# Wider column groups, a fifth buffer for high parts and later half tiles in the expert stage of an encoder kernel

## The reference, cut to what matters

```python
def _swiglu(h, w_gate_up, w_down):           # D_FF = 3584
    gu = h @ w_gate_up                       # [1024, 7168]: gate columns, then up columns
    g, u = gu[..., :D_FF], gu[..., D_FF:]
    return (jax.nn.silu(g) * u) @ w_down     # [3584, 1024]

for e in range(N_EXPERTS):                   # 8 experts
    y = y + gate_full[..., e:e + 1] * _swiglu(h, w_gate_up[e], w_down[e])
```

## Time and profile before

| | us |
|---|---|
| median of 3 runs (lowest, highest) | 1522.66 (1520.52, 1523.55) |
| the profiled execution | 1522.17 |
| its span | 1520.2 |
| TensorE busy | 1481.3 |
| VectorE busy | 1158.3 |
| ScalarE busy | 991.1 |

### The profile page before, as it was taken

One profiled execution on the slowest core, in us unless ns is written; L12 is line 12 of the kernel. 1 busy time (PEld: TensorE's weight loads), 2 busy tenths in 40 slices (PEclk: granted clock), 3 DMA queues, 4 the chain that ended last, 5 costly groups with the idle time before them and its releaser, 6 DMA issues.

```text
span 1520.2 us, 19543 instructions
## 1 busy us (share of the span) xinstructions
PE 1481.3 (97%) x7678; PEld 1208.7 (80%) x7678; DVE 1158.3 (76%) x1021; ACT 991.1 (65%) x869; POOL 132.2 (9%) x137
## 2 busy tenths in 40 slices
PE   8999999999989999999999999999999999999996
PEld 6888888899969987888777788777888777888774
DVE  5555445454565456899899988899898999898997
ACT  5544434343453337777798777888776888776986
POOL 0000000006034314000000200000100000000000
PEclk9999999999999999999999999999999999999999
DMA  9655555567516653899999999999999999999996
GB/s 333 214 170 190 168 192 171 189 192 224 194 57 213 206 185 126 329 356 355 366 405 417 398 407 405 395 408 415 399 408 403 395 408 415 399 404 408 393 391 220
DMA packets 151056, 468.26 MB, mean 308 GB/s; under 512 B 9856, under 2 KB 15872, under 8 KB 138416
## 3 DMA queue, kind: packets, MB, share of 16 engines
q1 hardware_dynamic: 144784, 453.93, 79.8%
q0 software_dynamic: 2816, 9.96, 2.3%
q10 hardware_dynamic: 3360, 3.06, 0.7%
HBM read 459.55 MB, written 7.37 MB: 307 GB/s over the span
## 4 chain that ended last, share of the span: by engine, by line
PE 79%; DVE 13%; ACT 3%; DMA 1%; SPq 1%; issue 1%; DVEq 0%; ACTq 0%
DVE wlo L418 9%; PE bS L437 6%; PE bS L438 6%; PE bS L436 6%; PE bY L436 6%; PE bY L438 6%; PE bY L437 6%; PE bG L436 4%; PE bG L438 4%; PE bU L436 4%; PE bG L437 4%; PE bU L438 4%; PE bU L437 4%; DVE wlo_more L418 2%; ACT whi L412 2%
## 5 line engine op out<-in xcount | busy, mean ns | idle before, releaser
L418 DVE TENSOR_TENSOR wlo<-raw,whi 128x2048 fp32r<-128x2048 f32 x364 | 827.2, 2296 | 179.6 <-ACT whi L412 178.4
L412 ACT ACTIVATE whi<-raw 128x2048 fp32r<-128x2048 f32 x364 | 692.3, 1915 | 262.1 <-PE bS L438 118.2
L418 DVE TENSOR_TENSOR wlo_more<-raw_more,whi 128x2048 fp32r<-128x2048 f32 x60 | 136.4, 2288 | 10.7 <-ACT whi L412 10.6
L412 ACT ACTIVATE whi<-raw_more 128x2048 fp32r<-128x2048 f32 x60 | 114.5, 1914 | 28.0 <-DMA raw_more<-in_m_w_gate_up_dram 8.4
L1086 PE MATMUL bY<-whi,hTh 128*128 128x512 f32 x224 | 91.5, 408 | 6.9 <-DVE wlo L418 4.9
L436 PE MATMUL bY<-whi,hTh 128*128 128x512 f32 x224 | 89.8, 401 | 0.0
L437 PE MATMUL bY<-whi,hTl 128*128 128x512 f32 x224 | 89.1, 398 | 0.0
L437 PE MATMUL bS<-whi,eTl 128*128 128x512 f32 x192 | 76.4, 398 | 0.0
L436 PE MATMUL bS<-whi,eTh 128*128 128x512 f32 x192 | 76.4, 398 | 0.0
L1086 PE MATMUL bS<-whi,eTh 128*128 128x512 f32 x192 | 76.3, 398 | 0.0
L1087 PE MATMUL bY<-wlo,hTh 128*128 128x512 f32 x184 | 73.2, 398 | 0.0
(11 more groups left out here) (536 smaller groups left out, 3336.4 us busy)
## 6 DMA issues: line engine op xcount, KB each, us to landing
raw<-in_m_w_gate_up_dram SPq DMA_DIRECT2D x184, 1024.0 KB, 14.5
raw<-in_m_w_down_dram SPq DMA_DIRECT2D x90, 1024.0 KB, 14.4
raw_more<-in_m_w_gate_up_dram SPq DMA_DIRECT2D x40, 1024.0 KB, 14.6
raw<-in_b_w_in_dram SPq DMA_DIRECT2D x36, 1024.0 KB, 5.1
raw<-in_f_w_gate_up_dram SPq DMA_DIRECT2D x28, 1024.0 KB, 5.2
raw_more<-in_m_w_down_dram SPq DMA_DIRECT2D x20, 1024.0 KB, 14.2
raw<-in_f_w_down_dram SPq DMA_DIRECT2D x14, 1024.0 KB, 5.0
raw<-in_a_w_out_dram SPq DMA_DIRECT2D x4, 1024.0 KB, 16.8
```

The costliest lines, as they stand in the source:

```text
L412: nc.scalar.activation(whi[:, h], raw_of(r), ACT.Copy).then_inc(hi_done, 1)
L418: nc.vector.tensor_tensor(wlo_of(r), raw_of(r), whi[:, h].bitcast(F32), ALU.subtract).then_inc(lo_done, 1)
```

## The change

Five edits go together, all in the expert stage.

1. **Groups of 2048 columns.** The 7168 columns are taken in order: three groups of 8 tiles, each tile 128 rows x 2048 columns (rows of 8 KB), into four banks G, S0, S1, U at once, then 4 tiles of 256 rows x 1024 columns (rows of 4 KB) into G and S0. Gate slabs 0 to 3 come from group 0, gates 4 to 6 and up 0 from group 1, ups 1 to 4 from group 2, ups 5 and 6 from the narrow tiles. Gates wait in a new area `parked` (over `hTl`). At each group change all four banks have to be evicted, each for itself (`gu_psum`, `column_sums`, `bank_free`), before PE writes it again.
2. **A fifth high buffer** `whi_late` (over `hn`, which is free by then), used from the seventh tile of item 0 on. `LEAD` = 4 takes the place of `CUT` = 3: splits run four tiles ahead.
3. **Evictions** stand in ACT's program behind the split at t = 6, 14, 22 (and 27), not behind t = 7, 15, 23.
4. **Turns** of slabs 0 to 6 stand in PE's program behind tiles 17, 24, 25, 27, 29, 31, 33, where they stood behind 9, 10, 17, 18, 25, 26 and 30 (half) or 31 (full).
5. **Last item:** the first 6 down tiles are whole (rows of 8 KB, both halves), the other 8 by half, 4 and 4. The left half is evicted once 10 down tiles are used and spread behind the 13th (before: 7, and the 11th).

The core of the diff:

```diff
 CUT = 3
+LEAD = 4
-PAIRS = SLABS // 2
-SINGLE = 8 * PAIRS
+GROUPS = 2 * FF // 2048
+NARROW = KD * GROUPS
+LAST_WIDE = 6
+LAST_HALF = 4
+UPS_OF = ((), (0,), (1, 2, 3, 4), (5, 6))
...
+        whi_late = place("whi_late", [2048], F32R)
...
+        parked = place("parked", [SLABS, 512], F32)
...
-            if t < SINGLE:
-                g, r = divmod(t, 8)
-                part, q = divmod(r, 4)
-                c = part * FF + g * 1024
-                return gate_up[q * 256:q * 256 + 256, c:c + 1024].rearrange("(k p) n -> p k n", p=P)
+            if t < NARROW:
+                g, kb = divmod(t, KD)
+                return gate_up[kb * P:kb * P + P, g * 2048:g * 2048 + 2048]
...
+        def hi_slot(t):
+            return t % HI if t < T_LATE else (0, HI, 1, 2, 3)[(t - T_LATE) % (HI + 1)]
+        def hi_free(t, item):
+            if isinstance(item, int) and in_order(t, item) > T_LATE:
+                return used_count(t, item, HI + 1)
+            return used_count(t, item, HI)
...
+        def column_sums(engine, n, g, s):
+            if s == (3 if g < GROUPS else 1):
+                engine.wait_ge(tile_used, count(n, FFN_TILES, T_MOE + (KD * g + KD if g < GROUPS else DOWN)))
+            else:
+                engine.wait_ge(gu_psum, count(n, 10, 3 * g + s + 1))
...
+                def bank_free(g, s):
+                    if g == 1:
+                        pe.wait_ge(gate_copied, count(k, SLABS, s + 1))
+                    if g == 2 and s < 3:
+                        pe.wait_ge(gate_copied, count(k, SLABS, s + 5))
+                    if g == 2 and s == 3:
+                        pe.wait_ge(up_copied, count(k, SLABS, 1))
+                    if g == 3:
+                        pe.wait_ge(up_copied, count(k, SLABS, s + 2))
...
+                turned = {18: 0, 25: 1, 26: 2, 28: 3, 30: 4, 32: 5, 34: 6}
+                for t in range(FFN_TILES):
+                    ahead(t)
+                    if t == 3:
+                        amid(0)
+                    if t in (6, 14):
+                        for j in range(4) if t == 6 else range(4, SLABS):
+                            copy_gate(j)
+                    if t in (14, 22, 27):
+                        copy_ups({14: 1, 22: 2, 27: 3}[t])
+                    if t in turned:
+                        slab_silu(turned[t])
+                    if t - 1 in turned:
+                        slab_hi(turned[t - 1])
```

More of the change, by code:

```diff
@@ new lines, in full_item @@
+                for t in range(DOWN):
+                    gate_up_product(t)
+                    if t in turns:
+                        turn(turns[t])
+                    if t in (3, 11, 25):
+                        amid(t // KD)
+                before_down()
+                for t in range(DOWN, FFN_TILES):
+                    pe.wait_ge(ht_lo, count(k, SLABS, PAIRS0 + (t - DOWN) // 2 + 1))
+                    down_product(t)
+                    if t in turns:
+                        turn(turns[t])
+                    if t == DOWN + 5:
@@ new lines, in gate_up_product @@
+                def gate_up_product(t):
+                    tile_ready(T_MOE + t, n)
+                    for s, blk, kb, stop in blocks_of(t, False):
+                        if t < KD:
+                            tokens_ready(n, kb, s)
+                        if kb == 0:
+                            bank_free(t // KD, s)
+                        w = wblk_backward(T_MOE + t, blk, n)
+                        pe.matmul(backward(gate_up_banks[s], 0, 512), eTh[:, kb], w[0], start=kb == 0, stop=False)
+                        mm = pe.matmul(backward(gate_up_banks[s], 0, 512), eTh[:, kb], w[1], start=False, stop=stop)
+                        if stop and s < (3 if t < NARROW else 1):
+                            mm.then_inc(gu_psum, 1)
+                    mm.then_inc(tile_used, 1)
@@ L1099, in turn @@
                             to = slice(part * 256 + c * HALF_CAP, part * 256 + (c + 1) * HALF_CAP)
[L1100 removed]
+                            mm = pe.matmul(bank[:, to], hidden_block(rows, c, by_half and j >= LAST_WIDE // 2), fold[:], start=True, stop=True)
                     mm.then_inc(jt_psum, 1)
[L1103 to L1114 removed]
@@ L1115, in half_item @@
[L1115 to L1122 removed]
+                turns = {17: 0, 24: 1, 25: 2, 27: 3, 29: 4, 31: 5, 33: 6}
+                for t in range(DOWN):
+                    gate_up_product(t)
+                    if t in turns:
+                        turn(turns[t])
+                    if t in (3, 11, 25):
+                        amid(t // KD)
@@ L1129, in half_item @@
-                    if t == DOWN + (0 if by_half else 2):
-                        turn(SLABS - 1)
+                    down_product(t)
+                    if t in turns:
+                        turn(turns[t])
                     if by_half and t in (DOWN + 7, DOWN + 9):
```

441 lines of the change are left out of this document (166 added, 275 removed).

## The result

The changed kernel takes 1524.87 us in the median of 20 runs (1521.47 to 1529.03), the kernel before, in the same job, 1522.38 us (1520.52 to 1525.18): a ratio of 1.0018, 95% interval 1.0011 to 1.0024. That is slower by 0.18%, inside what the prediction called no change, and 14 us from the 1511 forecast. The profiled execution took 1526.4 us (1522.2 before).

What follows compares the result with a forecast made beforehand. Full items were taken as bound by TensorE and half items by VectorE, the DMA just not the bound. 1522.2 - 6.6 (three halves) - 4.7 (last item) = 1510.9, with the median's 0.5 1511.4, said as 1511 us; range 1504 to 1522.

Steps and rivals of the forecast that it cites:

- no change: Whole kernel: a measurement can tell about 0.2%, 3 us, from no change; the chance given to "same" was 0.15.
- four banks at once: Group changes: PE does not wait for ScalarE's four evictions in a line if ScalarE stands ready; cost nothing.
- The bound of 1.5 us a change: Upper bound on four banks at once: each of 3 changes in each of 4 halves stalls VectorE.
- The slower rival: Halves: ScalarE late for its block of four, high parts run dry 1.5 us at 12 group changes; 1530 us, chance 0.14.
- Longer rows: Expert loads: 2.3 us less DMA time an item, lowering the pair's floor from 222.4 to 217.7 us; no gain by itself.
- Fifth buffer: Halves 1, 3, 5: one split less for VectorE, 2.2 us each, 6.6 in all; the longer rows are its cover.
- Turns late: Halves, tiles 24 to 33: PE drops 2.8 us behind and makes it up; nothing, bounds nothing and 2 us a half.
- Last item: Last expert item: loads need 3.7 us less, so it takes some 97 us, as a half does; 4.7 us gained.
- The left half's addition: Last item's end: added 1.41 us behind its spread, under PE's last tile as before; 0.63 us of VectorE's wait as cover.
- Share 1.02 in every window: DMA share in the expert stage, said to speak for the rival that the loads pace everything.
- the first rival: Expert stage: the loads pace everything, each microsecond of DMA time counts, 16.8 us gained; 1506 us median, chance 0.17.
- the tests that it named: Signs: halves 97 to 98 us, fulls 122 to 123, last item 97; wrong if PE waits at tiles 8, 16, 24.

Runs made afterwards that it cites:

- the test: On the changed kernel with the four up copies one split earlier in halves: 24 wide gate-up tiles an item loaded as 256 rows of 4 KB; 1527.99 us (1.0033).
- the test on the kernel before: Kernel before, 4 KB rows and evictions as they were, with only the fifth high buffer and splits four tiles ahead: 1521.83 us (0.9997).

## Why the prediction was wrong

By the profiles the span came out 15.6 us over the forecast: 7.4 us in the last item, 6.0 in the three halves, 1.0 each in the tail and ahead of item 1, 0.3 in the fulls. Two terms failed, the blocks of four and the last item.

**The step that failed: four banks at once, "cost nothing".** It argued that PE does not wait "if ScalarE stands ready, and the earlier place sees to that", and set ScalarE's program against PE's tiles and VectorE's splits. It left out the third thing ScalarE waits for. In half item 3 ScalarE entered the block 2.2 us after the banks were complete, held by the load and the high part of tile 26, and PE lost 2.9 us and 1.5 more at the lower clock. The bound of 1.5 us a change was too narrow for the change at tile 24, and at tiles 8 and 16 of halves 3 and 5 it was nearly free, as said. The slower rival had the place and the point of decision right (0.8 us late); it looked for the cause in VectorE's supply and not in a load, and it priced all 12 changes at once.

**Longer rows.** Right: 2.5 us a tile, and 8.8 us in the test, against 7 items x 1.7 = 12 as the most that its 24 wide tiles of an item could give. The test's own windows have 410 GB/s for 4 KB rows and 425 for 8 KB, much as the earlier trace rows had it; from landing to landing in half item 3 a wide tile took 2.56 us in the test and 2.49 in the changed kernel. Against that stands the 1.1% of the Trainium skill's rule (DMA: Bandwidth & Descriptors, Why small descriptors are slow), by which, as an estimate, 4 KB rows would cost 0.03 us a tile, 0.7 an item and 5 in the seven; they cost 8.8, so the measurement decides, with the caution that part of the 8.8 is blocks that came to stand behind later loads. What I overlooked is that the fourth tile of lead comes out of the lead of the loads: in half item 3 of the changed kernel most high parts of tiles 17 to 30 start the moment their load lands (1013.48 above is one); before the change the loads had landed 2 to 5 us ahead of the high part.

**Fifth buffer.** Right in place once the blocks are mended: the halves are 2.2 us shorter, the pair 220.0. Taken away by itself, beside blocks that all stand one up, it cost 1.4 us a half. Its cover, the rows, was named, and the test on the kernel before shows it. The slot costs nothing, as taken.

**Turns late.** Nothing in the halves, as taken: they reach 98.0 with them. In the last item it was wrong. I carried the half's figure over, but there the down order is another, and the seventh slab, with its low part behind the split of tile 39, is needed three tiles earlier than in the halves (37, not 40).

**Last item.** The term of -4.7 us failed, and it is the largest piece of the miss: it measured +2.7 in the change itself, +0.9 with the blocks of four ups and the first SiLU block mended, -0.2 with the last turns sooner. Loads did land 4.4 us earlier (last at 1499.7 against 1504.1), as the longer rows promised. PE ended 3.3 us later. "It then takes what a half takes now" assumed one bound for both. What the runs show in its place is two late evictions, the seventh slab behind the split of tile 39, and VectorE's row of splits; the 4 us that are still missing from 97.3 stay open.

**The left half's addition.** It came where it was expected: it started 1.8 us ahead of the end of PE's last matmul, before the change 1.5. What the prediction had not seen is what follows it. VectorE starts the statistics 1.98 us after the addition; before the change it started them 0.03 us after.

```profile
1508.72 0.69 DVE L2218 CUSTOM_DVE_ANT_0 squares<-x 128x512 f32<-128x512 f32 x1
```

After the change:

```profile
1510.34 1.41 DVE L2061 SCALAR_TENSOR_TENSOR x<-bS,gate_item,x 128x512 f32<-128x512 f32 x2 [4.42 <-PE bS L1046]
1513.73 0.69 DVE L2193 CUSTOM_DVE_ANT_0 squares<-x 128x512 f32<-128x512 f32 x1 [1.98 <-issue]
```

The tail grew by 1.0 us. The loop over overflow items stands between the two instructions. My reading is that before, when the addition waited for nothing, the sequencer was through the loop's control by the time it ran, and that now it stands at the addition's wait first. That is argued from the program and not shown; the spread one tile earlier takes 0.7 to 1.0 us off the tail and leaves the 1.98 us.

**Readings and sums.** "Share 1.02 in every window" does not hold for the last item, 0.96 in the earlier trace rows. Two rivals' sums are off by a rounding: 1.5 + 11.5 + 3.7 is 16.7, and 1522.2 - 11 + 18 is 1529. No more than the chance of the first rival hangs on them.

**Of the tests that it named,** PE's wait at tile 24 came up as written, and so did full items of 122 us. ScalarE's waits for loads were to be watched in the fulls; it was in the halves that one of them mattered.

## What to carry to other kernels

When work of an in-order engine is gathered into a block that another engine waits for, list everything that the engine waits for just ahead of the block, loads too, and ask which of it comes last once the change has made the stage faster. A block that two engines share is moved on both or on neither. Price a lead or a buffer together with its cover: here a kernel without the longer rows, without the buffer or with the block in the wrong place was slower than the kernel before (1.0033, 1.0051, 1.0018), and one with all three, and the SiLU block mended too, was 4 to 7 us faster.

## What was not expected of the hardware

- The clock. The changed kernel has five waits of 2.0 to 2.9 us for a bank. Behind four of them (793, 1016, 1442 and 1463 us) the granted clock was at the lower level for some eight matmuls (0.50 in the window above), at 793 us from the fourth matmul on, then 1.00 again; each such stretch cost some 1.5 us on top of the wait. Behind the fifth, 2.57 us at 1238, it stayed at the upper level, as it did behind a wait of 3.22 us at 1312 in the kernel with rows of 4 KB:

```profile
1238.50:1241.90 3.40, 3.37 (x21) 3.04 (x22) 2.82 (x3) 3.40 (x5) 0.00 (x0) 1.00 1.01 419
1312.30:1315.70 3.40, 3.37 (x15) 2.75 (x16) 1.95 (x2) 3.40 (x5) 0.00 (x0) 1.00 1.02 414
```

  So the length of a wait alone does not tell whether slow matmuls follow. Behind a wait of 1.29 us at 1053 us in the kernel before, matmuls came at 0.233.
- A load rate that is another engine's. Loads of 8 KB rows ran at about 420 GB/s with five or more in flight. At the end of full item 2, with two or three in flight, the windows have less, and the same for the changed kernel (first line) and for the one with rows of 4 KB (second):

```profile
945.00:965.00 20.00, 20.00 (x87) 16.12 (x86) 16.05 (x7) 13.84 (x10) 0.10 (x1) 1.00 0.99 371
945.00:965.00 20.00, 20.00 (x88) 16.07 (x87) 16.36 (x11) 13.84 (x8) 0.00 (x0) 1.00 0.99 371
```

  A load is issued there when PE frees a slot, every 2.80 us, and 1.0486 MB in 2.80 us is 374 GB/s. So this is PE's pace and says nothing of the rows, though the DMA share reads 0.99: a share near 1 does not show that the loads are the bound.
